# All eight branch tiles of the second group in the recurrence's block 0, and two more seven-product pairs

## The reference, cut to what matters

```python
proj = jnp.einsum('bsd,de->bse', x, w_in[l]) + b_in[l]
q, k, v, g_attn, x_rnn, g_rnn, m_attn, m_rnn = jnp.split(proj, split_at, axis=-1)
...
attn = _window_attention(q, k, v, attn_sink[l]) * jax.nn.silu(g_attn)
xc = _centred_depthwise_conv(x_rnn, conv_w[l], conv_b[l])
rnn = _bidirectional_rglru(xc, lru_wa[l], lru_ba[l], lru_wx[l], lru_bx[l],
                           lru_lambda[l]) * jax.nn.silu(g_rnn)
merged = (jax.nn.sigmoid(m_attn) * jnp.einsum('bse,ed->bsd', attn, w_branch_attn[l])
          + jax.nn.sigmoid(m_rnn) * jnp.einsum('bse,ed->bsd', rnn, w_branch_rnn[l]))
out = jnp.einsum('bsd,de->bse', merged, w_out[l]) + b_out[l]
x = _layernorm(ALPHA * x + out, ln_gain[l], ln_bias[l])
```

## Time and profile before

| | |
|---|---|
| median of 3 runs | 1029.24 us (1028.87 to 1029.38) |
| the profiled execution, its own time | 1029.07 us |
| its span, first to last instruction | 1027.3 us |
| TensorE (PE) busy | 1009.8 us |
| GpSimd (POOL) busy | 618.0 us |
| VectorE (DVE) busy | 670.9 us |
| ScalarE (ACT) busy | 471.8 us |
| stage of the recurrence's gates and pairs | about 394.8 to 822 us |

### The profile page before, as it was taken

How to read it: one execution, slowest core, us unless ns; L and a number is a source line. 1 busy time by engine, 2 the same in 40 slices (tenths; PEclk the granted TensorE clock), 3 DMA queues, 4 the chain that set the end, 5 groups by cost and what they waited for, 6 DMA issues and landing times.

```text
span 1027.3 us, 12975 instructions
## 1 busy us (share of the span) xinstructions
PE 1009.8 (98%) x4641; PEld 836.1 (81%) x4641; DVE 670.9 (65%) x769; ACT 471.8 (46%) x687; POOL 618.0 (60%) x378
## 2 busy tenths in 40 slices
PE   8999999999999999999999999999999999999997
PEld 6888888888888888878887888787887878888885
DVE  4946665503556653666587886877878488839756
ACT  4054445221554465573758466574856741102021
POOL 5654435446543422535499999999999734485223
PEclk9999999999999999999999999999999999999999
DMA  8264333565524121435262534435243788937012
GB/s 330 98 240 134 126 120 113 178 239 187 168 78 163 53 71 52 143 106 192 65 218 76 154 102 136 130 115 164 84 142 84 242 296 322 341 99 295 1 47 118
DMA packets 65861, 154.69 MB, mean 151 GB/s; under 512 B 6928, under 2 KB 7312, under 8 KB 65680
## 3 DMA queue, kind: packets, MB, share of 16 engines
q1 hardware_dynamic: 56880, 131.36, 38.7%
q10 hardware_dynamic: 8928, 22.64, 5.7%
HBM read 108.88 MB, written 45.09 MB: 150 GB/s over the span
## 4 chain that ended last, share of the span: by engine, by line
PE 83%; POOL 7%; DVE 4%; issue 3%; DMA 2%; ACT 1%; SPq 0%; DVEq 0%; POOLq 0%; ACTq 0%
PE proj L863 13%; PE proj L865 13%; PE proj L864 13%; PE proj L1067 6%; PE proj L1071 5%; PE proj L1073 5%; POOL w_lo L751 5%; PE aux L863 3%; PE aux L865 3%; PE aux L864 3%; PE aux L927 3%; PE aux L909 2%; POOL w_hi L764 2%; PE proj L1184 1%; PE proj L1183 1%
## 5 line engine op out<-in xcount | busy, mean ns | idle before, releaser
L716 POOL TENSOR_SCALAR w_hi<-raw 128x1024 fp32r<-128x1024 f32 (+1 forms) x46 | 62.5, 1358 | 246.1 <-PE proj L863 190.4
L863 PE MATMUL proj<-xt_hi,w_hi 128*128 128x512 f32 x476 | 192.2, 404 | 0.2
L865 PE MATMUL proj<-xt_hi,w_lo 128*128 128x512 f32 x476 | 186.4, 392 | 0.0
L864 PE MATMUL proj<-xt_lo,w_hi 128*128 128x512 f32 x476 | 186.2, 391 | 0.0
L751 POOL TENSOR_TENSOR w_lo<-raw,w_hi 128x512 fp32r<-128x512 f32 x66 | 123.7, 1879 | 4.4
L719 POOL TENSOR_TENSOR w_lo<-raw,w_hi 128x1024 fp32r<-128x1024 f32 (+1 forms) x46 | 123.4, 2682 | 3.8
L865 PEld LDWEIGHTS proj<-xt_hi,w_lo 128*128 128x128 f32 x476 | 89.3, 188 | 19.7
L863 PEld LDWEIGHTS proj<-xt_hi,w_hi 128*128 128x128 f32 x476 | 89.6, 188 | 15.7 <-DVE xt_lo L1604 0.8
L864 PEld LDWEIGHTS proj<-xt_lo,w_hi 128*128 128x128 f32 x476 | 89.6, 188 | 14.1
L1067 PE MATMUL proj<-xt_hi,w_hi 128*128 128x512 f32 x224 | 87.8, 392 | 1.5 <-POOL w_lo L751 1.5
L1073 PE MATMUL proj<-xt_hi,w_lo 128*128 128x512 f32 x224 | 87.2, 389 | 0.0
(11 more groups left out here) (199 smaller groups left out, 2467.6 us busy)
## 6 DMA issues: line engine op xcount, KB each, us to landing
raw<-stream SPq DMA_DIRECT2D x52, 512.0 KB, 4.2
presum_a<-stream SPq DMA_DIRECT2D x42, 256.0 KB, 2.9
sums<-presum_a SPq DMA_DIRECT2D x42, 256.0 KB, 2.0
raw<-sums SPq DMA_DIRECT2D x38, 256.0 KB, 2.8
spill<-part ACTq DMA_DIRECT2D x16, 512.0 KB, 3.1
merges<-stage_out ACTq DMA_DIRECT2D x32, 256.0 KB, 3.6
raw<-stream SPq DMA_DIRECT2D x31, 256.0 KB, 2.7
raw_half<-stream SPq DMA_DIRECT2D x21, 256.0 KB, 2.8
```

What stands on the lines that cost most here:

```text
L716: nc.gpsimd.tensor_scalar(hi, raw[:, raw_slot, cols], 1.0, 0.0, ALU.mult, ALU.add)\
L863: begun = nc.tensor.matmul(bank, wh, mov_hi, start=first, stop=False)
L864: nc.tensor.matmul(bank, wh, mov_lo, start=False, stop=False)
L865: return begun, nc.tensor.matmul(bank, wl, mov_hi, start=False, stop=last)
```

## The change

`PLAIN` becomes 1. Block 0 now has gates and all eight branch tiles. Block 1 has gates with the first quarter of plain x2 between their halves, the rest of x2, and then pair 0, which is x3 with g1. Block 2 has gates, pair 1 (x4 with g2) and pair 2 (the first merge gates), as the later blocks have; its first two products stand between the halves of its gates. g1, x3, g2 and x4 are no plain tiles any more, so there are 16 pairs and 112 products.

The queues of ScalarE and VectorE are written out for blocks 0 and 1. Loads: t1 and t2 are now loaded after the first four half units of pair 0 and after the last branch tile, and the loads of t3 and of block 2's gates follow in the queue. The slots of the last weight ring change parity, and `load_branch(0)` waits for `product_split` at two below the last in place of four. `PRESUMS` spreads 32 parts over the same units, where it spread 28.

```diff
-NAMES_B = (("x", 1), ("gates", 0), ("attn", 0), ("attn", 1), ("x", 2),
-           ("gates", 1), ("attn", 2), ("attn", 3), ("g", 1), ("x", 3), ("gates", 2), ("g", 2), ("x", 4))
+NAMES_B = (("x", 1), ("gates", 0), ("attn", 0), ("attn", 1), ("attn", 2), ("attn", 3), ("gates", 1), ("x", 2))
...
-PLAIN = 3
-TWINS = [(("merge", 0, 0), ("merge", 0, 1))]
+PLAIN = 1
+TWINS = []
 for _b in range(PLAIN, RNN_BLOCKS):
     if _b < RNN_BLOCKS - 1:
         TWINS.append((("x", _b + 2) if _b < RNN_BLOCKS - 2 else ("g", _b + 1), ("g", _b)))
-    TWINS.append((("merge", _b - 2, 0), ("merge", _b - 2, 1)))
+    if _b > PLAIN:
+        TWINS.append((("merge", _b - 2, 0), ("merge", _b - 2, 1)))
...
@@ sync: loads of pair 0
                     load_half(7 * q + i)
                     if i == 3 and q == 0:
+                        for step in range(2, 6):
+                            load_t(step)
+                    if i == (2 if q else 5) and q not in MERGES:
+                        load_gates(TWINS[q][1][1] + 1)
+                    if i == 5 and q == 0:
                         load_t3(0)
                         load_t3(1)
...
-            sp.wait_ge(product_split, PRODUCTS - 4)
+            sp.wait_ge(product_split, PRODUCTS - 2)
             load_branch(0)
...
@@ tensor: the loop over blocks, after
             for b in range(RNN_BLOCKS):
+                first = merge_of(b) if twin_of(b) is None else twin_of(b)
+                last_x = ("x", PLAIN + 1)
+                gates(b, 0)
+                if b == 0:
+                    branch(0, 0)
+                if b == PLAIN:
+                    for j in range(2):
+                        tile_slice(j, UNITS[last_x], RING[last_x] % 2, FILLS[last_x], 0)
+                if b > PLAIN:
+                    twin_product(first, 0)
+                if b == PLAIN + 1:
+                    twin_product(first, 1)
+                gates(b, 1)
+                if b == 0:
+                    for t in range(1, 8):
+                        branch(t // 4, t % 4)
+                if b == PLAIN:
+                    for j in range(2, KT):
+                        tile_slice(j, UNITS[last_x], RING[last_x] % 2, FILLS[last_x], 0)
+                    twin_product(first, 0)
                 if b >= PLAIN:
+                    for i in range(2 if b == PLAIN + 1 else 1, 7):
+                        twin_product(first, i)
+                if b > PLAIN and twin_of(b) is not None:
+                    for i in range(7):
                         twin_product(merge_of(b), i)
...
@@ scalar: block 1 of the recurrence, after
+            act.wait_ge(rnn_done, 1)
+            sigmoids(1, 0)
+            t_high(2)
+            t_high(3)
+            sigmoids(1, 1)
+            decay_tanh(1)
+            decay_exp(1)
+            t_high(4)
+            t_high(5)
+            decay_square(1, 0)
+            decay_square(1, 1)
+            roots(1)
+            pad_x(2, FILLS["x", 2])
+            early_copy(0, 0)
+            conv_begin(2, FILLS["x", 2])
+            early_copy(0, 1)
+            t3_high(0)
+            t3_high(1)
+            conv_high(2)
+            early_copy(0, 2)
+            early_copy(0, 3)
+            sigmoid_of(1)
+            store_state(1)
...
@@ vector: block 1 of the recurrence, after
+            gated_input(1)
+            t_low(2)
+            t_low(3)
+            one_less_decay(1, 0)
+            one_less_decay(1, 1)
+            scan_input(1)
+            t_low(4)
+            t_low(5)
+            scans(1)
+            for tap in range(1, CONV_W):
+                conv_tap(2, tap)
+            conv_low(2)
+            t3_low(0)
+            t3_low(1)
+            for number in range(4):
+                twin_sum(0, number)
+            silu_of(1)
+            gated_sum(1)
```

## The result

The changed kernel takes **1048.41 us** (median of 4 runs, 1046.68 to 1050.33), beside 1029.31 us for the kernel before on the same chip (4 runs): ratio 1.0185, 95% interval 1.0173 to 1.0198, or 19.1 us slower. The forecast was 1043.4 with a range of 1034 to 1053. The profiled execution took 1050.33 us, 1.9 above the median; its span is 1048.5 us, 21.2 over that of before.

A forecast was written before the change was run, and what follows sets the result against it. TensorE, busy 1009.8 of 1027.3 us, was taken as the bound, with GpSimd nearly level in steady blocks. From 1029.07 us: -5.4 + 15.3 + 2.9 - 1.9 + 2.0 + 1.4 = +14.3, so 1043.4 us, range 1034 to 1053.

The forecast's parts named there:

- the two stalls: Block 1: TensorE idle before product 1 of pair 0, some 7 us, and before product 6, some 7 to 8 more.
- the weight sums: Attention: 32 sum parts put two parts ahead of unit 18's split, 2.0 us (0 to 3.3); other places have room.
- The matmuls: Four plain tiles of 48 matmuls become two pairs of 84: 24 matmuls fewer, 5.4 us less.
- Product 1: Block 1, pair 0: waits for ScalarE's `pad_x(2)` behind the roots, at G+20.6, and starts some 7 us late.
- G: The start of `gates(1, 1)` in block 1, from which the prediction counts its times in us.
- Product 6: Block 1, pair 0: waits for `t3_low(1)` in VectorE's queue, starts at G+42.5, 15.3 us late (8.2 to 23).
- `gates(2, 1)`: Block 2's second half of gates waits for sigmoids behind pair 0's last product: 2.9 us (2.4 to 3.6).
- The clock: Block 1: the clock falls to 1.2 GHz in two new idle stretches; 1.4 us after the second (0 to 2.7).
- Splits in blocks 2 and 3: Of 4.1 us of waiting before, some 2.2 stay, 0.7 in block 3 and 1.5 in block 2: -1.9 us.
- the stretch: From the start of block 0's gates to block 4's: 780 matmuls in 181.02 us before, 4.1 us of it waiting.
- The wait at unit 18: Attention: unit 18's split ends at 254.5 to 256.0 us while TensorE wants it at 253.22; 2.0 us taken.
- stalls covered: Rival: block 1's stalls are covered, all together under 5 us, and the matmuls' time is gained: 1023.7 us, chance 0.06.

The follow-up runs named there:

- experiment 4: The changed kernel with ScalarE's copy of x2, `pad_x(2)`, put ahead of block 1's two squares: 1047.83 us, ratio 1.0181 to the kernel before.
- Experiment 6: The changed kernel with only ScalarE's and VectorE's orders in block 1 changed, copy of x2 and t3 work earlier: 1043.45 us, ratio 1.0145 to the kernel before.
- experiment 5: The changed kernel with 28 thrown-away matmuls ahead of product 6 of pair 0 to keep TensorE busy: 1046.71 us, ratio 1.0159 to the kernel before.
- the four others: Traces of four other kernels with the changed kernel's schedule up to `gates(0, 0)`, which started there between 399.10 and 400.67 us.
- experiment 1: The kernel before with 32 sum steps in the attention, the four extra stored and never read: 1034.68 us, ratio 1.0052 to the kernel before.
- experiment 3: The 32 sum steps placed otherwise: in the changed kernel 1043.39 us, ratio 1.0141; as control in the kernel before with 32 steps 1028.67 us, ratio 0.9989.
- 9: The changed kernel with reordered queues, later gates and other sum places, plus further queue moves on GpSimd, VectorE and ScalarE: 1038.03 us, ratio 1.0082 to the kernel before.
- experiment 10: The kernel of 9 with ScalarE instead of GpSimd making the high halves of products 4, 5 and 6 of pair 0: 1034.02 us, ratio 1.0046 to the kernel before.

## Why the prediction was right, and which term was mis-sized

The direction, the two stalls and their places were right; the time was 5.0 us short, inside the range. Two terms were mis-sized, and the larger part of the gap is the first, the weight sums. Against the profiled execution the forecast is 6.9 short: 4.9 in the attention, 1.3 from `gates(0, 0)` to `gates(4, 0)`, 0.6 in the rest.

- **The matmuls**, -5.4: 24 fewer, as said.
- **Product 1**, at G+20.0 with `pad_x` as releaser; forecast G+20.6.
- **Product 6**, at G+42.7; forecast G+42.5 by the medians. That the sum is so close is partly luck: the roots ended 0.5 us sooner than forecast, and behind them `t_low` took 3.8 us (3.1 forecast), the scans 4.8 (6.6), the taps 6.0 (4.7) and `t3_low` 3.8 (3.1). That experiment 4 ended at the same G+42.5 shows that the copy was no part of that sum: VectorE's queue sets it. Experiment 6 shows that the wait at product 6 was order and not load: with t3 ahead of the scans it was gone.
- **`gates(2, 1)`**: 2.1 measured, 2.9 forecast.
- **The clock**: 1.6 at product 6, 1.4 forecast; experiment 5 shows that the whole stretch wins only 0.55 us when it is taken away there. After the first stall 12 matmuls took 5.3 us in place of 2.7, hidden by the second, as forecast.
- **Splits in blocks 2 and 3**: 2.3 us of waits are left in the changed kernel from 520 to 595 (1.58 and three of 0.2 to 0.3), 2.2 forecast. But the term of -1.9 was wrong. It took 4.1 us of waiting in the stretch of before, which is the stretch less the pace of its matmuls; TensorE was idle for only 2.35 of them (181.02 less 178.67), and this line gives its waits there:

```profile
PE proj L1067 <- POOL w_lo L751: 2.1, 3, 1.7
```

  So nothing was won: about 0 in place of -1.9.
- Together the stretch lost 13.6; the terms for it were -5.4 + 15.3 + 2.9 - 1.9 + 1.4 = 12.3. The term of the splits accounts for the gap, less 0.8 at `gates(2, 1)`.
- **The weight sums**: forecast 2.0 (0 to 3.3), measured 6.9 in this trace and 4.3 to 5.9 in the four others, 5.8 by experiment 1 and 4.5 to 5.0 by experiment 3. The wait at unit 18 was there, 2.28 us, with the split from 254.18 to 257.67, so that part was right. The step that failed is that everything else was put at nothing, by the sentence "The extra bytes and sums themselves lie in GpSimd's idle time". The number of steps did cost nothing; but shifting the parts changed which of VectorE's instructions had GpSimd beside them, and TensorE waits for the queries and the row maxima behind these. The ten starts of the rotary sum came 0.8, 0.6, 0.6, 0.7, 1.3, 2.1, 2.1, 5.6, 7.7 and 6.9 us later than in the kernel before. The first 0.7 cost nothing, as experiment 3 has it too. The steps to 1.3 and 2.1 each follow an `at_lo` of 1.78 us in place of 0.69 and a wait of 0.4 for `neg_max`. The jump of 3.5 holds the wait at unit 18, the next of 2.1 the rotary sum of 2.33 us in place of 1.22, with waits of 1.06 and 0.98 behind it. That the longer instructions cause these waits is read from the traces; no run changed them alone.

The rival "stalls covered" asked whether an order exists in which they are: the runs built most of one, and the gain of 5.4 still didn't come. What stood behind the stalls, and what no term of mine counted, is GpSimd's pace: of seven splits two are made ahead, and the other five take 3.4 to 3.8 us each, against products of 2.72. Besides, the longest waits that were left (2.3 to 5.4 us) had matmuls at the slow clock behind them, which cost 4.4 us in experiment 6, 3.2 in 9 and 1.4 in 10, by the distances between starts. The forecast needed no term for GpSimd, because the stalls gave it the time. Whether a version with more of the high halves on ScalarE, in pair 1 as well, would beat the kernel before wasn't tried.

## What to carry to other kernels

When work is spread anew over an engine's idle time, check what its neighbour does in the new places: the number of sum steps cost nothing, their places about 5 us. Where a stall has one visible releaser, work out when the next three inputs are ready before counting on its removal: the copy, t2, t3, GpSimd's splits and the next gates each stood ready to take over, and of 12.5 us of waits at two products, reordering won 4 to 5. A denser stage (fewer matmuls for the same weights) needs its feeders' pace compared first: 3.8 us a product against 2.72.

## What the hardware showed that I had not expected

Where GpSimd and VectorE worked side by side, instructions of both took 1.8 to 2.6 times as long. A 128x512 high half took GpSimd 0.61 us at the quickest and 1.59 with VectorE busy all along, a sum step 1.29 and 2.28, while VectorE's 128x1024 `rot_a` went from 1.22 to 2.33 and the 128x512 `at_lo` from 0.68 to 1.78. The slow clock cost 1.6 us after an idle stretch of 6.3 us with a granted clock of 0.50, as seven matmuls ran slowly before it was back. It also fell after shorter waits: after 2.34 us in experiment 10 six matmuls started 0.43 us apart, and after 2.05 us in experiment 5 the granted clock was 0.54, while after 2.06 us in the changed kernel it stayed at 1.00.
